# Eight expert slots, norms kept in PSUM, and smaller moves at the joints of a two-block transformer kernel

## The reference

```python
# first block
proj = rms_norm(h, norm1_g) @ w_in             # q k v qi ki wi su sv ga gb
y_attn = dsa_attention(rope(q), rope(k), v, rope(qi), rope(ki), wi)   # 8 heads, top 64 keys
y_sgu  = spatial_gating(gelu(su), gelu(sv), ...)
merged = sigmoid(ga) * (y_sgu @ w_branch_a) + sigmoid(gb) * (y_attn @ w_branch_b)
h = h + merged @ w_out
h = h + hier_moe(rms_norm(h, norm2_g), ...)    # 32 experts, 2 for each token
h = rms_norm(h, norm_f_g)
# second block: layer 0 window attention, layer 1 gated linear attention (HGRN2)
for layer in (0, 1):
    y = mixer(rmsnorm(h, g[layer, 0]), mem_kv[layer])   # each with cross attention to a memory
    h = h + rmsnorm(y, g[layer, 1])
    f = conv_ffn(rmsnorm(h, g[layer, 2]), ...)          # 1024 -> 2 x 2816 -> 1024
    h = h + rmsnorm(f, g[layer, 3])
```

## Time and profile before

| | us |
|---|---|
| median of three runs | 1441.32 (1439.64 to 1446.77) |
| profiled execution | 1439.86 |
| its span | 1437.90 |
| PE busy | 1268.1 (88%) |
| POOL busy | 782.5 (54%) |
| ACT busy | 632.9 (44%) |
| DVE busy | 548.7 (38%) |
| moved by DMA | 275.00 MB, mean 191 GB/s |

### The profile page before, as it was taken

One profiled execution on the slowest core, in us unless ns is written; L12 is line 12 of the kernel. 1 busy time (PEld: TensorE's weight loads), 2 busy tenths in 40 slices (PEclk: granted clock), 3 DMA queues, 4 the chain that ended last, 5 costly groups with the idle time before them and its releaser, 6 DMA issues.

```text
span 1437.9 us, 19440 instructions
## 1 busy us (share of the span) xinstructions
PE 1268.1 (88%) x7815; PEld 1054.2 (73%) x7815; DVE 548.7 (38%) x1006; ACT 632.9 (44%) x1060; POOL 782.5 (54%) x347
## 2 busy tenths in 40 slices
PE   5999999885887777897889999999899789699997
PEld 4878877764533344586768999988798687599986
DVE  3729653433111121234642222203447971333211
ACT  4445543532111111453645645535589432555441
POOL 4779974520000000495006988878668903588884
PEclk9999999996999999999999999999999999899999
DMA  6545545253799999754004555455434422455541
GB/s 225 159 164 176 210 152 193 77 212 137 281 410 410 409 410 410 297 183 154 30 1 163 176 189 176 164 179 186 162 125 166 153 97 70 138 189 189 178 175 74
DMA packets 138331, 275.00 MB, mean 191 GB/s; under 512 B 7380, under 2 KB 53772, under 8 KB 138252
## 3 DMA queue, kind: packets, MB, share of 16 engines
q1 hardware_dynamic: 137980, 272.87, 52.8%
q10 hardware_dynamic: 272, 1.05, 0.2%
HBM read 272.85 MB, written 1.05 MB: 190 GB/s over the span
## 4 chain that ended last, share of the span: by engine, by line
PE 68%; ACT 9%; DVE 9%; DMA 7%; POOL 3%; issue 3%; SPq 1%; DVEq 0%; ACTq 0%
PE lin_ps L809 10%; PE lin_ps L810 10%; PE lin_ps L811 10%; PE lin_ps L829 7%; PE lin_ps L832 7%; PE lin_ps L831 7%; DMA ring<-in_w_expert_in 3%; PE lin_ps L1033 3%; ACT w_high L1278 3%; POOL w_low L740 3%; PE sc_ps L1047 3%; PE lin_ps L1061 2%; DMA ring<-in_w_mem_kv 1%; PE tr_ps L1070 1%; PE sc_ps L883 1%
## 5 line engine op out<-in xcount | busy, mean ns | idle before, releaser
L740 POOL TENSOR_TENSOR w_low<-ring,w_high 128x1024 fp32r<-128x1024 f32 (+1 forms) x320 | 773.5, 2453 | 638.3 <-ACT w_high L1278 638.2
L1278 ACT ACTIVATE w_high<-ring 128x1024 fp32r<-128x1024 f32 (+1 forms) x320 | 311.8, 1040 | 152.2 <-PE lin_ps L811 86.1
L829 PE MATMUL lin_ps<-x_high,w_high 128*128 128x256 f32 x960 | 273.0, 284 | 3.9 <-DVE cross_low L601 2.6
L831 PE MATMUL lin_ps<-x_high,w_low 128*128 128x256 f32 x960 | 272.4, 284 | 0.0
L832 PE MATMUL lin_ps<-x_low,w_high 128*128 128x256 f32 x736 | 208.3, 283 | 0.0
L829 PEld LDWEIGHTS lin_ps<-x_high,w_high 128*128 128x128 f32 x960 | 185.0, 193 | 4.4 <-DVE cross_low L601 2.8
L809 PE MATMUL lin_ps<-w_high,x_high 128*128 128x512 f32 (+1 forms) x464 | 184.3, 397 | 3.7 <-POOL w_low L740 2.6
L831 PEld LDWEIGHTS lin_ps<-x_high,w_low 128*128 128x128 f32 x960 | 185.0, 193 | 0.1
L810 PE MATMUL lin_ps<-w_low,x_high 128*128 128x512 f32 (+1 forms) x464 | 181.9, 392 | 0.0
L811 PE MATMUL lin_ps<-w_high,x_low 128*128 128x512 f32 (+1 forms) x400 | 156.6, 392 | 0.0
L832 PEld LDWEIGHTS lin_ps<-x_low,w_high 128*128 128x128 f32 x736 | 141.3, 192 | 0.0
(11 more groups left out here) (354 smaller groups left out, 1970.0 us busy)
## 6 DMA issues: line engine op xcount, KB each, us to landing
ring<-in_w_expert_in SPq DMA_DIRECT2D x32, 2048.0 KB, 16.2
ring<-in_ffn_w_in SPq DMA_DIRECT2D x44, 1024.0 KB, 7.8
ring<-in_w_expert_out SPq DMA_DIRECT2D x16, 2048.0 KB, 19.6
ring<-in_w_in SPq DMA_DIRECT2D x15, 2048.0 KB, 7.8
ring<-in_b_w_in SPq DMA_DIRECT2D x11, 2048.0 KB, 8.0
ring<-in_ffn_w_out SPq DMA_DIRECT2D x8, 2048.0 KB, 8.0
ring<-in_w_mem_kv SPq DMA_DIRECT2D x4, 2048.0 KB, 10.7
ring<-in_a_w_in SPq DMA_DIRECT2D x4, 2048.0 KB, 7.9
```

What stands on the lines that cost most here:

```text
L740: pool.tensor_tensor(w_low[:, slot, 0:words], raw, w_high[:, slot, 0:words].bitcast(F32), ALU.subtract).then_inc(low_made, 1)
L829: pe.matmul(out, wh[:, j, at], high(k), start=(k == 0 and f < 2), stop=False, skip_group_check=True)
L831: pe.matmul(out, wl[:, j, at], high(k), start=False, stop=False, skip_group_check=True)
L1278: act.activation(w_high[:, slot, 0:words], raw, ACT.Copy).then_inc(high_made, 1)
```

## The change

The expert loop has eight slots: 0 to 3 for the first weights, 4 and 5 for the second weights of even passes, and two more in `work` (buffers 2 and 3, 7 and 8) for those of odd passes. All engines run the loop over pairs of passes with the two written out. SP loads the second weights of pass 1 ahead of the loop. The router's weights and the normalized rows are stored in another order of features (feature 8 f + k at k, f), so that the gather and the router read adjacent columns, and the norm ahead reads every eighth.

Branches are multiplied and added in PSUM, the first half of `merged` is turned within the second branch block, the second half within w_out0. `attention` on ACT has a begun form; the first exponentials of the window attention stand ahead of the copy of a3, those of the second cross attention ahead of the copy of b4, its first scores stand within b4, and the turning of its results within b5. Post-norms keep the product with the gain in PSUM (`sc_ps` for the first half, in place for the second); the first half's sum is made into a bias, so that two roots follow the second half's squares; `h` is updated in four halves, each squared at once on ACT. In the o1 norm the splits of the next block's units stand behind. The tables of levels 4, 3 and 2 are copied by ACT to PSUM and pair 0 reads them there.

```diff
-LOAD_ORDER = (0, 1, 2, 4, 3, 5)
+EXPERT_SLOTS = 8
...
+                order = "(p k) n -> p k n" if name == "router" else "(k p) n -> p k n"
...
+        first_mult_at = {2: (sc_ps, 0), 3: (sc_ps, NB), 4: (tr_ps, 0)}
...
+        def expert_slot(j):
+            if j < RING:
+                return ring[:, j, :]
+            return work[:, 2048 * (2, 7)[j - RING]:2048 * (2, 7)[j - RING] + SLOT]
...
-                expert_loads(0, last_use)
-                with sp.Fori(1, BATCHES) as b:
-                    expert_loads(b, lambda j: sp.wait_ge(expert_used[j], b))
+                sp.wait_ge(x_low_made, split_groups["y"] + 8)
+                load_second(1, 1, 0)
+                for j in (0, 1, 2):
+                    last_use(j)
+                    load_first(0, j)
+                last_use(4)
+                load_second(0, 0, 0)
+                pieces_used(sp, router_piece - 3)
+                sp.wait_ge(x_low_made, split_groups["mem"] + 8)
+                load_second(1, 1, 1)
+                last_use(3)
+                load_first(0, 3)
+                last_use(5)
+                load_second(0, 0, 1)
+                for j in range(4):
+                    sp.wait_ge(expert_used[j], 1)
+                    load_first(1, j)
...
+                for parity in range(2):
+                    for f in range(2):
+                        second_when_free(1, parity, f)
+                    for j in range(4):
+                        first_when_free(1, parity, j)
+                with sp.Fori(2, BATCHES // 2) as pair:
+                    for parity in range(2):
+                        for j in range(3):
+                            first_when_free(pair, parity, j)
+                        second_when_free(pair, parity, 0)
+                        first_when_free(pair, parity, 3)
+                        second_when_free(pair, parity, 1)
...
-            for j in range(2):
-                linear(f"w_branch_b{j}", *parts(x_high, x_low7), ready=made("y"))
-            pe.wait_ge(merged_ready, 2)
-            turn_split("merged", 8, merged)
-            linear("w_out0", *parts(x_high, x_low7), ready=made("merged"))
+            linear("w_branch_b0", *parts(x_high, x_low7), ready=made("y"))
+            linear("w_branch_b1", *parts(x_high, x_low7),
+                   ready=amid(6, lambda: pe.wait_ge(merged_ready, 1), lambda: turn_split("merged", 4, merged)))
+            def merged_parts(k):
+                if k == 2:
+                    pe.wait_ge(merged_ready, 2)
+                    turn_split("merged", 8, merged, first=4)
+                parts_made(pe, "merged", k + 1)
+            linear("w_out0", *parts(merged_high, merged_low), ready=merged_parts)
...
-                                mm = pe.matmul(gather_ps[:, k, :], scaled[:, t, :].rearrange("p (f k) -> p k f", k=KC)[:, k], picks[:, t, :],
+                                mm = pe.matmul(gather_ps[:, k, :], scaled[:, t, P * k:P * (k + 1)], picks[:, t, :],
...
-            linear_turned("b4", *from_x)
-            cross(1)
-            turn_split("cat1", 4, x_out1)
+            linear_turned("b4", *from_x, ready=amid(5, lambda: cross(1, begun=False)))
+            cross(1, begun=True)
+            linear_turned("b5", *from_x, ready=amid(3, cross_results))
...
+            def norm_root_by_halves(nth, i):
+                if i < len(NORMS):
+                    for t in range(TILES):
+                        for j in range(2):
+                            act.wait_ge(half_in, 2 * TILES * nth + 2 * t + j + 1)
+                            step(act.activation(attn[:, NB * (2 * t + j):NB * (2 * t + j + 1)], h[:, t, NB * j:NB * (j + 1)],
+                                                ACT.Square, accum_out=half_sq[:, t, j:j + 1]))
+                            if j == 0:
+                                step(act.activation(half_bias[:, t:t + 1], half_sq[:, t, 0:1], ACT.Identity, scale=1.0 / D,
+                                                    bias=eps[:]))
...
+            attention("att0", ATT_HEADS, True, begun=False)
             copy_turned("a3", four(xqT))
-            attention("att0", ATT_HEADS, True)
+            attention("att0", ATT_HEADS, True, begun=True)
...
+            act.wait_ge(hg_tables, 1)
+            for level in (4, 3, 2):
+                (held, at), (dst, dst_at) = mult_at[level], first_mult_at[level]
+                act.activation(grid(dst, dst_at, (1, 4 * MULT)), grid(held, at, (1, 4 * MULT)), ACT.Copy)\
+                    .then_inc(hg_tables_moved, 1)
...
-                dve.tensor_tensor(merged[:, :, cut], merged[:, :, cut], gb[:, :, cut], ALU.add).then_inc(merged_ready, 1)
+                dve.tensor_tensor(merged[:, :, cut], ps, merged[:, :, cut], ALU.add).then_inc(merged_ready, 1)
...
-                for t in range(TILES):
-                    ins = dve.scalar_tensor_tensor(h[:, t], x[:, t], small[:, 6 + t:7 + t], h[:, t], ALU.mult, ALU.add)
+                for t in range(TILES):
+                    for j in range(2):
+                        part = slice(NB * j, NB * (j + 1))
+                        dve.scalar_tensor_tensor(h[:, t, part], held[j][:, t, :], small[:, 6 + t:7 + t], h[:, t, part],
+                                                 ALU.mult, ALU.add).then_inc(half_in, 1)
```

More of the change, by code:

```diff
@@ L594, in take_high, with take_low @@
                     .then_inc(x_high_made, 1)
[L596 to L598 removed]
+        def take_low(dve, name, n, high, low, gain_name=None, first=0):
+            for i in range(first, n):
                 dve.wait_ge(x_high_made, split_groups[name] + i + 1)
@@ L849, in turn, with turn_split @@
                     mm.then_inc(tr_done, 1)
-            def turn_split(name, n, src):
-                for i in range(n):
+            def turn_split(name, n, src, first=0):
+                for i in range(first, n):
                     if i >= 4:
@@ L1388, in _ @@
             take_high(act, "y", 8, x_high)
+            split_units(sum(units[piece("w_out1")]) - 1)
+            take_high(act, "merged", 4, merged_high)
             split_to(piece("w_out1"))
-            take_high(act, "merged", 8, x_high)
+            take_high(act, "merged", 8, merged_high, first=4)
             act.wait_ge(mem_in, 16)
@@ L1562, in _ @@
             act.wait_ge(hg_dec, 1)
-            for j in range(2):
-                copy_block(f"b{8 + j}", half(hgate, j), ACT.Silu)
+            copy_block("b8", half(hgate, 0), ACT.Silu)
+            act.wait_ge(hg_tables, 1)
[3 more added lines that the diff above has]
+                    .then_inc(hg_tables_moved, 1)
+            copy_block("b9", half(hgate, 1), ACT.Silu)
             for j in range(2):
```

341 lines of the change are left out of this document (197 added, 144 removed).

## The result

The changed kernel takes 1402.56 us (median; 1399.68 to 1404.40) against 1442.42 us in the same comparison: ratio 0.9716, 95% interval 0.9699 to 0.9733. That is 1.8 us under the forecast of 1404.4. The profiled run took 1404.40 us with a span of 1402.7, 35.2 us less than before, where 36.9 were predicted.

A forecast was written before the change was run, and what follows sets the result against it. TensorE, busy 88% of the span, bounds the kernel, level with transfers in the expert loop. Terms 12.7 - 0.5 + 5.6 + 2.6 + 4.1 + 4.3 + 5.8 + 1.5 + 0.75 = 36.9 us give median 1404.4; 80% range 1393 to 1420.

The forecast's parts named there:

- Part 1, loop: Expert loop: two loads moved ahead save 10.2 us, the shorter gather 2.5; 12.7 us, between 0 and 14.2.
- the transfers end the stage: Expert loop: with the gather shorter, passes of 25.6 us stay under the 30.7 that six loads cost.
- the second rival, *late feed: ACT and POOL make weight units too late once 16.6 us of stalls go; 1421 if all given back; chance 0.16.
- Norm ahead of the router: Norm ahead of the router reads every eighth number, which costs 0.5 us, bounds 0 and 1.5.
- the sum of 36.3 with both: Total gain if both tiles' slower norm ahead of the router were on the path, 1.1 us, instead of 36.9.
- Part 2, merge: Merge of the branches: TensorE's 4.65 us wait for DVE and the ramp behind go; 5.6 us, bounds 4.0 and 7.0.
- the ramp behind it (about 1 us): Merge: the ramp behind TensorE's wait for DVE goes with that wait, about 1 us.
- Part 3: Attention ends: earlier exponentials in the first group, 2.6 us; scores and turns moved in the second cross attention, 4.1 us.
- Part 4, tables: First pair's level products fall to 0.42 us with one factor in PSUM; 4.3 us, bounds 3.0 and 6.5.
- Part 5: Norms behind the blocks: o1 5.8 us, the two of layer 0 1.5 together, the last norm 0.75.
- The gather shrank: Answers the rival for the expert loop that the gather does not shrink: 12.7 us come back, 1417; chance 0.17.
- The clock in the loop: Rival: waits for transfers lower the clock in the expert loop; at 0.60, 61 us more, 1466; chance 0.07.

The follow-up runs named there:

- e6: Changed kernel with the splits of the next block's units ahead of the squares in o1's norm again; 1404.9 us, ratio 0.9722.
- e2: Changed kernel with the old strided gather, norm ahead of the router and router rows, eight slots kept; 1409.8 us, ratio 0.9772.
- e1: Kernel before with only the gather from adjacent numbers and norm and router rows to match, six expert slots; 1441.9 us, ratio 0.9993.
- e4: Changed kernel with the product of the branches written to SBUF and added from there; 1405.2 us, ratio 0.9745.
- e8: Changed kernel with a ninth expert slot in the attention scratch and first-product loads ahead of second ones from pass 5; 1398.0 us, ratio 0.9679.
- e11: Changed kernel with the gained output of o1 held in SBUF instead of PSUM until added to h; 1403.9 us, ratio 0.9726.
- e12: Changed kernel with a ninth expert slot but its own load order in passes 5 to 8; 1398.7 us, ratio 0.9690.
- e9: Changed kernel with the second layer's cross attention wholly as before, b5 waiting for the splits; 1409.2 us, ratio 0.9771.
- e3: Changed kernel with the first pair's level products reading the factor tables in SBUF, copies to PSUM kept; 1408.7 us, ratio 0.9763.

## Why the prediction was right, and where not

**The total** was right partly by cancelling: the loop and o1 gave 6.2 us less than their terms, the merge, the cross attention and the tables 5.7 more.

**Part 1, loop: 12.7 predicted, 8.5 measured.** The mechanism held: transfers end the stage, and they do so two pieces earlier. The first load behind the loop's start comes 9.3 us after it instead of 10.9, and transfers run, by windows of 3 and 5 us, from 363.3 to 579.0 instead of 370.8 to 596.7: 17.7 us earlier at their end, of which 10.2 are the two pieces. The step that failed is "the transfers end the stage": TensorE cannot follow their end. In the last pass the fourth piece comes at 565.99, and 15.05 us of work stand behind it, 1.7 of them lower clock; kv00 starts at 581.04, not 579. Another 1.45 us goes inside kv00, where GpSimd makes four units in 9.44 us and then waits for ACT, which has the norm's squares in front: 22.74 us to u0's turn instead of 21.29. That is the second rival, *late feed*, in a mild form. So 1.6 for the gather and 10.3 for the pieces, less 2.1 and 1.45, make 8.4. (In e6, the same loop, kv00's part was 21.30 and the whole 248.19, so these two losses are not fixed.) "Eight passes make 236.5 us" was wrong in the old kernel already: they took 238.7, the last ones at the pace of the transfers (e2). And the reading that the gather took 7.92 us at both levels of the clock did not follow from its two rows, which both have a fall inside them; it is true all the same, as the gather at 446.73 shows (7.89 us at 1.00).

**Norm ahead of the router: 0.5 predicted, 0.4 measured** (wait 5.26 against 4.87 in e2, 5.62 against 5.24 in e1). Each tile takes 1.15 us instead of 0.75, which agrees with the rule on 16-byte lines in the Trainium skill, SBUF — State Buffer, section "Door 1: The DMA port swizzle". Only one tile is on the path, so the sum of 36.3 with both was not needed. The table does not show the 0.4, since the changed kernel gave as much back at the same wait: DVE goes on 0.11 us behind ACT's second root where it was 0.47 before. Why, I have not found.

**Part 2, merge: 5.6 predicted, 7.3 measured and 1.5 given back behind it.** No wait is left, and the clock, at 0.66 from 296 to 306 before, is at 1.00. The step that was mis-sized is "the ramp behind it (about 1 us)": by the matmul that started at 301.07 before, 5.4 us are gained, and in the rest of the old fall and just behind it (to 304.66) another 1.8. I had capped the gain at 7. The 1.5 is a fall in w_out1, which had 1.00 before. First 5 us of that block by windows, before and after:

```profile
317.67:322.67 5.00, 5.00 (x22) 4.18 (x23) 0.00 (x0) 0.00 (x0) 0.00 (x0) 1.00 1.02 419
```

```profile
310.39:315.39 5.00, 5.00 (x16) 4.00 (x17) 0.00 (x0) 0.00 (x0) 0.00 (x0) 0.69 1.02 416
```

I cannot tie it to the edit: with the wait (before, e1, e4) it was absent three times of three, without it present in seven executions and absent in four (e6, e8, e11, e12).

**Part 3.** First attention: 2.6 predicted; the first profile gave 3.9 for a stretch with o0's norm in it; eleven executions average 162.2 against 164.9 for the two of the old code, 2.6 for both edits together, where I had 2.6 and 0.75. With a scatter of 6 us between single executions that difference is not shown. The wait of 5.46 became one of 2.81 for ACT's copy, as the step said. Cross attention: 4.1 predicted, 6.8 measured. At the first product of b5 (1035.69 before) 5.2 us are gained, where I had placed 4.1. The rest, 1.65, is the lower clock behind the gap, for which I counted nothing; in e9 it is 2.7.

**Part 4, tables: 4.3 predicted, 5.6 measured.** Products at 0.42 us with GpSimd busy, next late ACT's near keys: both as said. TensorE goes on 4.1 us behind the pair's first products (1117.33 to 1121.44), at the moment the keys end, where I had put 5.0 (1143.19 to 1148.2). The same matmul stood at 1151.81 before, so 4.5 us are gained there. What I left out is again the clock: behind the old wait it was at 0.50 from 1149.72 to 1156.55. These are the same matmuls, before and after:

```profile
1151.81:1155.33 3.52, 3.52 (x47) 3.46 (x46) 0.12 (x1) 0.82 (x3) 1.10 (x1) 0.50 1.05 403
```

```profile
1121.44:1123.38 1.94, 1.94 (x46) 1.90 (x46) 0.00 (x0) 0.36 (x1) 1.94 (x2) 1.00 0.84 259
```

That is 1.6 us more, and TensorE gives 0.5 of it back in a longer wait for DVE at 1125.17.

**Part 5.** o1: 5.8 predicted, 5.3 without and 3.8 with a fall of the clock inside the block. DVE's part was right (2.7 us for 2.48); the wait behind o1 is 8.7, where I had said near 8. By e6 and e11 the late splits and PSUM are worth 1.7 each. The norms of layer 0: 0.9 for fo0's, o0's cannot be told from the attention's scatter. The last norm: 0.75 predicted; from the last squares on 0.46 came, and the stretch as a whole gave nothing, since its first matmuls, behind the wait of o1, spend 0.4 us more at the lower clock than before.

**The rivals.** The gather shrank (e1). The feed was late in one place only. The clock in the loop did not fall further: six falls before, three after. But the three cost 1.7 us each and the six nothing (e2). They come behind the long waits, 4.88, 3.33 and 3.20 us, in the last three passes. The Trainium skill, TensorE: Matmul & The Clock Gate, section "HAM oscillation — how this bites in real kernels", says that a wait for transfers in each block lets the next begin cold; the trace agrees for these three, but shows no fall behind a wait of 3.18 us at 448.23; in e6 the same wait, at 446.94, has one.

## What to carry to other kernels

Where two sides of a stage are near level, shortening either alone buys little (0.6 and 2.9 us) and both together much more (8.5). Look for scratch that is idle in such a stage: one more prefetched piece was worth about 5 us here. An operand of DVE moved to PSUM took 2.1 us off at each of three places where GpSimd works beside it, and paid where TensorE waited for that result (5.6 us for the tables, 2.0 and 1.7 for the merge and o1). And when you price a wait that is to go, read the clock behind it: it was worth another 1.8, 1.65 and 1.6 us at the merge, the cross attention and the tables, and counting it as 1 us or nothing is the larger part of what was mis-sized there.

## What was unexpected of the hardware

A fall of the granted clock to 0.50 cost 1.4 to 1.7 us where products followed each other (o1 block, w_out1, the loop after), and nothing within the strided gather (7.9 us with it and without). At two joints it comes or stays away in executions of the same instructions with the same idle times in front (o1 block: five of ten). Differences under 2 us at one place of one profile therefore prove nothing about an edit.

How small a DVE instruction can be and still be held up by GpSimd. Before (GpSimd busy to 1233.6, and the same instruction at the kernel's end with GpSimd idle), and after (GpSimd busy from 1174.1 to 1188.3):

```profile
1229.66 1.65 DVE L1969 TENSOR_TENSOR small<-post_sq 128x2 f32<-128x2 f32 x1 [0.24 <-DVE work L1966]
1231.73 0.17 DVE L1971 RECIPROCAL small<-small 128x2 f32<-128x2 f32 x1 [0.42 <-ACT small L1444]
1431.34 0.16 DVE L1969 TENSOR_TENSOR small<-post_sq 128x2 f32<-128x2 f32 x1 [0.24 <-DVE work L1966]
```

```profile
1181.29 2.33 DVE L2092 TENSOR_SCALAR post_bias<-post_sq 128x2 f32<-128x2 f32 x1
```

Two numbers a partition cost as much as a GpSimd unit (mean 2.45 us) has left to run: both instructions end within 0.03 us of the end of a unit. A reciprocal of the same size is not held. The delays of the large instructions fit one unit each: 2.1 us on an add (e4), 2.1 on a product (e3), 2.1 on four adds beside one unit (e11). The Trainium skill, SBUF — State Buffer, section "Who interferes with whom", says that a DVE instruction with two SBUF inputs contends with a GpSimd instruction that reads SBUF, and that `tensor_scalar` can enter a form with two ports in which whichever engine comes second is blocked for the whole instruction. The trace agrees with both: L1969 has two inputs, and L2092 is a `tensor_scalar` with one. That L2092 ran in this form is not shown; that it was held is.
